# Tokens split at 320 instead of 288, with the high and low parts of the other 256 in one product of 512 columns

## The reference

```python
for i in range(DEPTH):                                  # DEPTH = 2
    xn = rms_norm(x, norm_mix[i])
    y = rglru_mixer(xn, ...) if i == 0 else mlstm_mixer(xn, ...)
    x = x + y
    x = x + swiglu(rms_norm(x, norm_ffn[i]), ffn_w_up[i], ffn_w_down[i])   # 1024 -> 2 x 2816 -> 1024
    gate = jax.nn.sigmoid(x @ ple_w_gate[i] + ple_b_gate[i])
    x = x + gate * (p[i] @ ple_w_proj[i])
y = rms_norm(x, norm_final)
```

## Time and profile before

| | |
|---|---|
| median of 3 runs | 2071.94 us (2070.14 to 2074.52) |
| the profiled execution | 2070.35 us |
| its span, first to last instruction | 2068.6 us |
| mean granted TensorE clock | 0.966 of full speed |
| TensorE busy | 1953.5 us (94%) |
| VectorE / ScalarE / GpSimd busy | 714.0 / 739.8 / 817.3 us |

### The profile page before, as it was taken

The page is one execution under the profiler, slowest core; times in us unless marked ns, Lnnn a source line. Parts: engine busy times, 40 slices in busy tenths (PEclk is TensorE's granted clock), DMA queues, the critical chain, the costliest instruction groups (busy, mean ns, idle before and its releaser), DMA issues.

```text
span 2068.6 us, 35513 instructions
## 1 busy us (share of the span) xinstructions
PE 1953.5 (94%) x13543; PEld 1797.2 (87%) x13543; DVE 714.0 (35%) x801; ACT 739.8 (36%) x1096; POOL 817.3 (40%) x659
## 2 busy tenths in 40 slices
PE   6999799999999999997898999999999999999997
PEld 6999799999999999994564655699999999999996
DVE  5677522111111113664545454532222111111213
ACT  3576633322222334334232414341443312222332
POOL 4233355544444435550010100253564544544433
PEclk8999999999999999998899889999999999999998
DMA  4222132222222224220657393722232222222212
GB/s 118 72 83 89 45 104 77 82 86 82 83 83 83 80 68 91 69 61 0 216 181 252 108 315 125 244 78 71 82 93 82 81 82 81 81 84 79 82 61 76
DMA packets 184818, 207.53 MB, mean 100 GB/s; under 512 B 23051, under 2 KB 148627, under 8 KB 184663
## 3 DMA queue, kind: packets, MB, share of 16 engines
q1 hardware_dynamic: 184066, 205.52, 32.1%
q10 hardware_dynamic: 648, 0.59, 0.1%
HBM read 165.44 MB, written 40.62 MB: 100 GB/s over the span
## 4 chain that ended last, share of the span: by engine, by line
PE 77%; issue 6%; DVE 6%; POOL 4%; ACT 4%; DMA 2%; ACTq 0%; POOLq 0%; DVEq 0%; SPq 0%
PE ps L1962 63%; POOL W_LO L603 3%; PE ps L2230 2%; PE ps L2180 2%; PE ps L2255 1%; PE ps L2119 1%; DVE C_HALVES L1808 1%; POOL SQUARE_SUM L611 1%; DVE H_PAD L1559 1%; DVE SQUARE_SUM L1854 1%; PE ps L2126 1%; PE ps L2212 1%; DMA out_ml_C_s_dram<-C_HALVES 1%; PE ps L2222 1%; PE ps L2145 0%
## 5 line engine op out<-in xcount | busy, mean ns | idle before, releaser
L603 POOL TENSOR_TENSOR W_LO<-W_RAW,W_HI 128x512 fp32r<-128x512 f32 x464 | 609.7, 1324 | 689.7 <-ACT W_HI L901 689.5
L901 ACT ACTIVATE W_HI<-W_RAW 128x512 fp32r<-128x512 f32 x484 | 297.9, 628 | 729.2 <-PE ps L1962 722.4
L1962 PE MATMUL ps<-A_HI,W_HI 128*128 128x288 f32 x2304 | 497.5, 298 | 15.7 <-POOL W_LO L603 7.1
L1962 PE MATMUL ps<-A_LO,W_HI 128*128 128x288 f32 x2304 | 495.5, 297 | 0.0
L1962 PE MATMUL ps<-A_HI,W_LO 128*128 128x288 f32 x2304 | 495.3, 297 | 0.0
L1962 PEld LDWEIGHTS ps<-A_HI,W_HI 128*128 128x128 f32 x2304 | 373.3, 190 | 18.4 <-issue 14.5
L1962 PEld LDWEIGHTS ps<-A_HI,W_LO 128*128 128x128 f32 x2304 | 373.4, 190 | 0.0
L1962 PEld LDWEIGHTS ps<-A_LO,W_HI 128*128 128x128 f32 x2304 | 373.4, 190 | 0.0
L1610 DVE TENSOR_TENSOR X<-X,ps 128x1152 f32 (+1 forms) x36 | 48.7, 1354 | 335.6 <-PE ps L1962 335.6
L1962 PE MATMUL ps<-G_HI,W_HI 128*128 128x288 f32 x704 | 150.9, 296 | 2.5 <-POOL G_LO L712 2.5
L1962 PE MATMUL ps<-G_HI,W_LO 128*128 128x288 f32 x704 | 150.8, 296 | 0.0
(11 more groups left out here) (358 smaller groups left out, 2430.5 us busy)
## 6 DMA issues: line engine op xcount, KB each, us to landing
W_RAW<-in_ffn_w_up_dram SPq DMA_DIRECT2D x176, 256.0 KB, 2.8
C_HALVES<-in_state_mlstm_C_dram SPq DMA_DIRECT2D x64, 512.0 KB, 5.4
out_ml_C_s_dram<-C_HALVES SPq DMA_DIRECT2D x64, 512.0 KB, 5.7
W_RAW<-in_ffn_w_down_dram SPq DMA_DIRECT2D x88, 256.0 KB, 2.7
W_RAW<-in_ml_w_in_dram SPq DMA_DIRECT2D x64, 256.0 KB, 2.8
W_RAW<-in_rg_w_in_dram SPq DMA_DIRECT2D x48, 256.0 KB, 2.7
W_RAW<-in_ple_w_gate_dram SPq DMA_DIRECT2D x32, 256.0 KB, 2.7
W_RAW<-in_ml_w_out_dram SPq DMA_DIRECT2D x32, 256.0 KB, 2.8
```

What stands on the lines that cost most here:

```text
L603: pool.tensor_tensor(W_LO[:, s], W_RAW[:, s], W_HI[:, s].bitcast(F32), ALU.subtract).then_inc(lo_ready, 1)
L901: act.activation(W_HI[:, s], W_RAW[:, s], ACT.Copy).then_inc(hi_ready, 1)
L1962: ins = pe.matmul(ps[:, 4 * s + 2 * m + h, 0:HALF_T], a[:, w, k, wc], x[:, h * HALF_T:h * HALF_T + HALF_T], start=i == 0 and k == 0 and q ...
```

## The change

Every job divides its tokens at WIDE = 320 instead of 288: 320 in the first bank of a pair, REST = 256 in the second. The high and low parts of an operand become two slices of one tensor (A_PARTS and so on), so that a moving operand can run over both. In a job that isn't `plain`, W_HI x high and W_HI x low of the 256 tokens are one product of 512 columns, into the two halves of the second bank; W_LO x high is added onto the first half. The two halves are added when the bank is read. A `plain` job keeps them apart, six products as before (320, 320, 256, 256, 320, 256) and one half of the bank. Plain are the convolution-branch jobs and the gate jobs of the RG-LRU, both kinds of the ple jobs, the mLSTM's input jobs and every second one of its output-gate jobs.

```diff
-            def job(s, pairs, operand, before=None, first=0, last=None, own=False):
+            def job(s, pairs, operand, before=None, first=0, last=None, own=False, plain=False):
...
-                            for q, (a, x) in enumerate(((W_HI, hi), (W_HI, lo), (W_LO, hi))):
-                                for h in range(2):
-                                    ins = pe.matmul(ps[:, 4 * s + 2 * m + h, 0:HALF_T], a[:, w, k, wc], x[:, h * HALF_T:h * HALF_T + HALF_T],
-                                                    start=i == 0 and k == 0 and q == 0,
-                                                    stop=i == pairs - 1 and k == 1 and q == 2)
+                            w_hi, w_lo = W_HI[:, w, k, wc], W_LO[:, w, k, wc]
+                            wide, rest = ps[:, 4 * s + 2 * m, 0:WIDE], ps[:, 4 * s + 2 * m + 1, 0:REST]
+                            both = ps[:, 4 * s + 2 * m + 1, 0:2 * REST].rearrange("p (l n) -> p l n", l=2)
+                            pe.matmul(wide, w_hi, hi[:, 0:WIDE], start=opens, stop=False)
+                            pe.matmul(wide, w_hi, lo[:, 0:WIDE], start=False, stop=False)
+                            if plain:
+                                pe.matmul(rest, w_hi, hi[:, WIDE:T], start=opens, stop=False)
+                                pe.matmul(rest, w_hi, lo[:, WIDE:T], start=False, stop=False)
+                            else:
+                                pe.matmul(both, w_hi, x[:, :, WIDE:T], start=opens, stop=closes, skip_group_check=True)
+                            pe.matmul(wide, w_lo, hi[:, 0:WIDE], start=False, stop=closes)
+                            ins = pe.matmul(rest, w_lo, hi[:, WIDE:T], start=False, stop=closes, skip_group_check=not plain)
```

VectorE's readers of such banks (link() makes VectorE wait for its own instruction):

```diff
+            def scaled(dst, s):
+                link(dve.tensor_reduce(rest(dst), ps_parts(s), mybir.AxisListType.X, ALU.add))
+                dve.tensor_tensor(wide(dst), ps_wide(s), R_WIDE, ALU.mult)
+                return dve.tensor_tensor(rest(dst), rest(dst), R_REST, ALU.mult)
...
-                dve.tensor_tensor(pair5(GELU_T[:, :, :]), psv[:, 1, :, :, 0:HALF_T], RB, ALU.mult).then_inc(psum_freed[1], 1)
+                scaled(GELU_T, 1).then_inc(psum_freed[1], 1)
...
-                xx = pair4(X[:, ds(c0, 2), :])
-                dve.tensor_tensor(xx, xx, psum4(s), ALU.add).then_inc(psum_freed[s], 1)
+                xx = X[:, ds(c0, 2), :]
+                link(dve.tensor_tensor(rest(xx), rest(xx), ps_rest(s), ALU.add))
+                dve.tensor_tensor(wide(xx), wide(xx), ps_wide(s), ALU.add)
+                dve.tensor_tensor(rest(xx), rest(xx), ps_more(s), ALU.add).then_inc(psum_freed[s], 1)
...
-                        dve.tensor_tensor(pair5(GATE[:, :, :]), psv[:, 0, :, :, 0:HALF_T], RB, ALU.mult).then_inc(psum_freed[0], 1)
+                        scaled(GATE, 0).then_inc(psum_freed[0], 1)
...
-                        link(dve.tensor_tensor(pair5(GATED[:, :, :]), psv[:, 1, :, :, 0:HALF_T], pair5(GATE[:, :, :]), ALU.mult))
+                        link(dve.tensor_reduce(rest(GATED), ps_parts(1), mybir.AxisListType.X, ALU.add))
+                        dve.tensor_tensor(wide(GATED), ps_wide(1), wide(GATE), ALU.mult)
+                        link(dve.tensor_tensor(rest(GATED), rest(GATED), rest(GATE), ALU.mult))
```

ScalarE's readers of two token halves in one instruction become two instructions, of 320 and 256 tokens: in gate_r and gate_i of the RG-LRU and in the sigmoid of ple (for each of two channel blocks), and in the copies to P_PROJ. For example:

```diff
-                    ins = act.activation(R_GATE[:, m].rearrange("p (h n) -> p h n", h=2), psv[:, slot, m, :, 0:HALF_T],
-                                         ACT.Sigmoid, bias=VECS1[:, C_BR + 2 * b + m:C_BR + 2 * b + m + 1])
+                    act.activation(R_GATE[:, m, 0:WIDE], psv[:, slot, m, 0, 0:WIDE], ACT.Sigmoid, bias=bias)
+                    ins = act.activation(R_GATE[:, m, WIDE:T], psv[:, slot, m, 1, 0:REST], ACT.Sigmoid, bias=bias)
```

More of the change, by code:

```diff
@@ L1126, in ple @@
                     act.wait_ge(slab_used, jobs.adv() + 2 * RING)
[L1127 removed]
+                    act.activation(wide(P_PROJ[:, 2 * m:2 * m + 2, :]), ps_wide(s), ACT.Copy)
+                    act.activation(rest(P_PROJ[:, 2 * m:2 * m + 2, :]), ps_rest(s), ACT.Copy).then_inc(psum_freed[s], 1)
                 act.wait_ge(acc_clear, acc0)
@@ L1623, in ffn @@
                 for g, (g0, gn) in enumerate(GROUPS):
-                    with loop(dve, gn // 2, {jobs: 8, uses[0]: 1, uses[1]: 1, blk: 1, ys: 1, step: 1}) as j:
+                    with loop(dve, gn // 2, {jobs: 8, uses[0]: 1, uses[1]: 1, blk: 1, ys: 1, step: 3}) as j:
                         b = blk.adv()
@@ L1640, in ffn @@
                     last = g == len(GROUPS) - 1
-                    with loop(dve, 4 // n, {jobs: ks * n, uses[0]: n // 2, uses[1]: n // 2, hi_t: n if last else 0}) as j:
+                    with loop(dve, 4 // n, {jobs: ks * n, uses[0]: n // 2, uses[1]: n // 2, step: n, hi_t: n if last else 0}) as j:
                         for m in range(n):
@@ L1885, in _ @@
                     states()
-                with loop(dve, 2, {jobs: 8, uses[0]: 1, uses[1]: 1, blk: 2, ys: 2}) as j:
+                with loop(dve, 2, {jobs: 8, uses[0]: 1, uses[1]: 1, blk: 2, ys: 2, step: 1}) as j:
                     for m in range(2):
@@ L1900, in _ @@
                 if not g:
-                    square_mean(HEADS - 1, [(4 + i, 288, 192 * i, 192) for i in range(3)])
+                    square_mean(HEADS - 1, [(b, c0, 192 * i, 192) for i, (b, c0) in enumerate(((4, WIDE), (5, REST), (6, WIDE)))])
                     normalise(HEADS - 1)
-                with loop(dve, 2, {jobs: 8, uses[0]: 1, uses[1]: 1, **({hi_t: 2} if g else {})}) as j:
+                with loop(dve, 2, {jobs: 8, uses[0]: 1, uses[1]: 1, step: 2, **({hi_t: 2} if g else {})}) as j:
                     for m in range(2):
@@ L2051, in turn_out, with ple @@
                 ins.then_inc(misc_done, 1)
-            def ple(layer, P_HI, P_LO, hi, lo, acc, xn0):
+            def ple(layer, x, acc, xn0):
                 pe.wait_ge(p_loaded, 32 * (layer + 1))
@@ L2062, in ple @@
                 for m in range(4):
-                    job((m + 1) % 2, 1, chunks(P_HI, P_LO))
+                    job((m + 1) % 2, 1, chunks(P_PARTS), plain=True)
                 with loop(pe, 2, {slabs: 8, uses[0]: 1, uses[1]: 1}) as j:
                     for m in range(2):
-                        job((m + 1) % 2, 4, chunks(hi, lo), lambda i: pe.wait_ge(xn_ready, xn0 + i + 1))
+                        job((m + 1) % 2, 4, chunks(x), lambda i: pe.wait_ge(xn_ready, xn0 + i + 1), plain=True)
                 if layer:
@@ L2076, in ple @@
                     ins.then_inc(misc_done, 1)
-            ffn(A_HI, A_LO, G_HI, G_LO, 8, 4)
-            ple(0, P_HI, P_LO, A_HI, A_LO, None, 8)
-            job(0, 4, chunks(B_HI, B_LO), starts(12, 12))
-            job(1, 4, chunks(B_HI, B_LO))
+            ffn(A_PARTS, G_PARTS, 8, 4)
+            ple(0, A_PARTS, None, 8)
+            job(0, 4, chunks(B_PARTS), starts(12, 12), plain=True)
+            job(1, 4, chunks(B_PARTS), plain=True)
             with loop(pe, 3, {slabs: 8, uses[0]: 1, uses[1]: 1}) as j:
                 for s in range(2):
-                    job(s, 4, chunks(B_HI, B_LO))
+                    job(s, 4, chunks(B_PARTS), plain=True)
             taken = [0]
```

138 lines of the change are left out of this document (80 added, 58 removed).

## The result

The changed kernel takes 2083.1 us (median of 11 runs, 2076.65 to 2085.11), the kernel before in the same comparison 2071.71 (2069.01 to 2078.52). The ratio is 1.0049, 95% interval 1.0036 to 1.0061: slower by 0.5%, some 10 us, where the forecast said 2064. The time lies inside the range given, on the other side of the kernel before. The profiled execution took 2080.92 us (span 2079.2), 10.6 us more than that of before.

The account below looks back on a forecast made before the run. TensorE, by the pace of L1962's products, was taken as the bound. -17.9 + 3.0 + 1.9 + 0.9 + 2.8 + 1.6 = -7.7 us from 2070.35 gives 2062.7, plus 1.6 to the median: 2064, range 2055 to 2085.

Parts of the forecast that it names:

- The removed product, 13.3 ns a group: TensorE's groups in jobs not plain: five products for six save 13.3 ns each, 17.9 us over 336 slabs.
- the rival: TensorE's products: the extra goes with columns, a removed product is worth under 7.6 ns, total 2082, slower; chance 0.17 with seam.
- The seam at nothing: 512-column product: the join between its moving operand's two runs costs nothing, at worst 13.3 ns.
- The reduction by what it reads, 1.23 us: VectorE adding the bank's halves in scaled(): priced by the 1024 elements read, 1.23 us, not 0.70 by those written.
- add_to_x in sum: VectorE's add_to_x in three pieces (512 + 640 + 512) takes 2.23 us, +0.95 with a link, instead of one 1.35.
- The first stage: RG-LRU: next W_LO just covered despite longer scaled(); ScalarE's split gates add 5 x 0.4 and 0.8, 2.8 us.
- dearer readers: Rival: reduction or links slower, group-end cover gone, first stage's W_LO late 0.5 a block; 8 us more, 2072; chance 0.05.
- Last group of each feed-forward, 1.5 each: Three-slab jobs: the last GATED delays TensorE by 1.4 and 0.1 us, twice, 3.0 us.
- Embedding +0.95 each: Feed-forward to per-layer embedding: P_HI waits behind the longer add_to_x, +0.95 twice, 1.9 us.
- States 0.9: Ahead of states(): the same wait for the longer add_to_x adds 0.9 us.
- The norm's cover: Norm ahead of a feed-forward: 2.4 us of cover hides add_to_x's +0.95, so nothing is added.
- The embedding's sigmoids, 1.6: Per-layer embedding: ScalarE's split reads, +0.4 a job, on the chain at three waits of layer 0 and the end, 1.6 us.

Follow-up runs that it names:

- experiment 4: Three measurement kernels, 24 forms of the product group each (780 to 806.7 ns for six of 288), then whole kernels with reordered products: 0.9940 to 1.0019 times the kernel before.

## Why the prediction was wrong, point by point

- **The removed product, 13.3 ns a group: the step that failed on size.** It measured 6.7 (793.3 for 800), and between the kernel with six products and the same readers and the changed one 8.5 us of the forecast 17.9. The prediction had reasoned that the extra goes with the product because it vanishes at the slow clock and is small for fp32. That the extra doesn't grow in proportion to the columns was right (five of 320 take 13.3 more each, five of 512 too), and the five prices alone would have given the forecast's 786.7; together, in this order, they cost 793.3. What it lacked: one length in one order can't show a constant, and I had said so of the rival ("the trace can't separate the two") without holding it against my own value. I had also ruled out, from rows of other products, that it matters whether two products go into one bank or into different ones; the orders of experiment 4 change just that, and they run at 780 to 806.7 ns. The rival's point, 7.6 ns, lay just above what came, and its total, 2082, is near the measured 2083.1; that is luck: the rival has no gain in the products and 2.8 us in the first stage, the runs show 8.5 and 10.6.
- **The seam at nothing: right**, shown by the contiguous operand.
- **The reduction by what it reads, 1.23 us: right** (1.225). add_to_x in sum 0.69 + 0.82 + 0.68 = 2.19: right (2.23).
- **The first stage: the step that failed on mechanism.** "scaled() at 164.09 puts the next W_LO to about 167.5 [...]: just covered." The changed kernel waits 1.28 us a block for it; the stage loses 10.6 us where I had 2.8. The order of VectorE's work was right, its prices weren't: I took the multiplication at 0.70 and W_LO at 0.68, the price of both where GpSimd doesn't read SBUF beside them, and they took 1.14 and 1.77. With my prices the cover would have held. I had left out that the longer reading puts both behind the start of GpSimd's W_LO. The same step passed over the first block, where the earlier trace rows don't reach: a wait that was there already (2.14 us) grew to 3.47, and with the slower clock behind it the block loses 2.7 us. What I put down to ScalarE's gates is 2.2 us, of the 2.8 said. A step whose spare time I put at zero had no price for the case that it failed, beyond the 0.5 us a block among the "dearer readers".
- **Last group of each feed-forward, 1.5 each.** TensorE's idle before the third slab is 2.38 us, from 1.22, so +1.16 where I had 1.5; but the first of the two costs 2.7 with the gain taken out, the second 1.2. The clock explains it; by stretches of the changed kernel right behind the two waits:

```profile
724.96:727.96 3.00, 3.00 (x10) 2.80 (x11) 0.00 (x0) 0.00 (x0) 2.42 (x2) 0.50 0.16 49
...
1948.04:1951.00 2.96, 2.96 (x18) 2.83 (x19) 0.00 (x0) 0.00 (x0) 2.44 (x2) 1.00 0.18 53
```

  After the same wait of 2.38 us the first has a granted clock of 0.50 (1.2 GHz) for 3 us, ten products where full clock does some twenty: 1.5 us more. Before, TensorE idled 1.22 us there and stayed at full clock. The idle time alone doesn't decide it: in six of the experiments' executions with these waits of 2.3 to 2.4 us, the clock fell behind the first in three, behind the second in one, behind both in one and behind neither in one. In the kernel with the plain GELU job it also fell in the first block, behind a wait of 2.2 us.
- **Embedding +0.95 each:** the idle is 5.02 us, from 4.22; the delay +0.9 and +1.4. States 0.9: +0.85. The norm's cover held.
- **The embedding's sigmoids, 1.6:** on the chain only in part; the stretch has +0.2 in layer 0, and the end of the kernel +0.3.

With 6.7 ns and the first stage's 10.6 the sum is: -9.0 (336 slabs), +10.6, +3.9 for the last groups, +2.3 at the embeddings and +0.9 for the states, 8.7 together; the table has +10.3, and 1.6 us stay unassigned.

## What to carry to other kernels

Price a removed instruction from two lengths or two orders of it, not from one; where the trace has only one, the range must run from nothing, and a change that pays for it with work elsewhere is a loss until shown otherwise. Where a reader of a bank grows, look at what stands behind it in the same engine's order and who waits for that, and take it at the price that it has beside GpSimd's work. A wait that grows can cost more than its own length, when the clock falls behind it. When an engine-bound loop has n operations of equal length, try their order before their number: here it cost nothing and gave about as much, though not in every execution.

## What the runs showed of the hardware

- At full clock an fp32r product with its weight load, in groups of one length from 256 columns on, takes its columns and 11.7 (288) to 20 ns (448) more: 504 and 512 columns both take 226.7. 128 and 192 both take 111.7.
- The same sequence of products can run at 780, 790, 800 or 806.7 ns a group at one granted clock, for hundreds of microseconds each.
- A VectorE instruction with both inputs in SBUF gets longer beside GpSimd's when it begins behind it: W_LO takes 0.68 us alone or 0.01 us ahead of GpSimd's W_LO, 1.76 to 1.78 behind it. The multiplication of scaled() that reads SBUF alone takes 0.68 in the 25 places of the changed kernel where GpSimd is idle or through within 0.1 us, 0.96 to 1.59 in the other 7. What reads PSUM keeps its time beside GpSimd: the reduction 1.22, the 640 elements 0.82. The rows of GpSimd in the changed kernel:

```profile
137.84 3.00 POOL L621 TENSOR_TENSOR W_LO<-W_RAW,W_HI 128x512 fp32r<-128x512 f32 x2 [1.75 <-ACT W_HI L919]
```

  The Trainium skill (SBUF — State Buffer, Who interferes with whom) states it: a VectorE instruction with two SBUF inputs contends with a GpSimd instruction that reads SBUF, one with at most one SBUF input doesn't. By that rule, the trace agrees: of the instructions beside GpSimd's from 137.84 to 140.84 only the two with both inputs in SBUF are long, and moving an operand from the bank to SBUF, as scaled() does, brings an instruction under it. No run here moves GpSimd's work away; the reading rests on the traces.
